# Compression and attention-gate weights read unsplit, as plain fp32 on four 32-column groups of the array

## What is computed

```python
DEPTH = 2
for l in range(DEPTH):
    h = rms_norm_2(x, norm_mix_pre[l])
    proj = h @ w_in[l]
    a_q, a_kv, a_gate, d_q, d_kv, b_in, c_in = jnp.split(proj, splits, axis=-1)
    ...
    k_cmp = nsa_compress(kv[:, :, 0, 0], nsa_cmp_pos[l, 0], nsa_cmp_w1[l, 0], nsa_cmp_w2[l, 0])
    v_cmp = nsa_compress(kv[:, :, 0, 1], nsa_cmp_pos[l, 1], nsa_cmp_w1[l, 1], nsa_cmp_w2[l, 1])
    o_cmp, p_cmp = nsa_compressed_attention(qa, k_cmp, v_cmp)
    ...
    ga = jax.nn.sigmoid(a_gate)          # 24 columns: 3 kinds x 8 heads
    o_a = ga[:, :, 0] * o_cmp + ga[:, :, 1] * o_slc + ga[:, :, 2] * o_win

def nsa_compress(k, pos, w1, w2):        # 15 blocks of 32 keys, stride 16, 2 key groups
    blk = k[:, idx] + pos
    flat = blk.reshape(bsz, n_cmp, g, 32 * 64)
    return gelu(flat @ w1) @ w2          # w1 is 2048 x 256
```

## Time and profile before

| | |
|---|---|
| median of three runs | 2051.24 us (2049.7 to 2053.11) |
| profiled execution, span | 2053.3 us |
| TensorE matmul busy | 2039.6 us, 99% |
| VectorE busy | 1475.2 us, 72% |
| ScalarE busy | 1152.8 us, 56% |
| chain that ended last | TensorE 96%, VectorE 1%, ScalarE 1%, DMA 1% |
| mean DMA rate | 180 GB/s |

### The profile page before, as it was taken

The page is one execution under the profiler, slowest core; times in us unless marked ns, Lnnn a source line. Parts: engine busy times, 40 slices in busy tenths (PEclk is TensorE's granted clock), DMA queues, the critical chain, the costliest instruction groups (busy, mean ns, idle before and its releaser), DMA issues.

```text
span 2053.3 us, 39877 instructions
## 1 busy us (share of the span) xinstructions
PE 2039.6 (99%) x17337; PEld 1975.7 (96%) x17340; DVE 1475.2 (72%) x1877; ACT 1152.8 (56%) x1459; POOL 129.9 (6%) x114
## 2 busy tenths in 40 slices
PE   9999999999999999999999999999999999999998
PEld 8999899999999999999999999999999999999998
DVE  6556866655655587676557999678778899868776
ACT  5435365534544456564446776756557685756555
POOL 1001000100101010010000000001000000000100
PEclk9999999999999999999999999999999999999999
DMA  7665544666566565366665554455655564445652
GB/s 256 206 206 175 183 144 141 196 198 195 175 207 200 190 193 165 103 200 221 223 200 168 163 165 140 159 175 186 223 191 156 162 199 160 149 151 171 222 186 103
DMA packets 287106, 369.78 MB, mean 180 GB/s; under 512 B 10531, under 2 KB 258771, under 8 KB 286931
## 3 DMA queue, kind: packets, MB, share of 16 engines
q1 hardware_dynamic: 281858, 361.47, 54.1%
q10 hardware_dynamic: 5072, 5.75, 0.9%
HBM read 365.36 MB, written 1.05 MB: 178 GB/s over the span
## 4 chain that ended last, share of the span: by engine, by line
PE 96%; DVE 1%; ACT 1%; DMA 1%; ACTq 0%; issue 0%; DVEq 0%
PE ps L717 28%; PE ps L718 27%; PE ps L719 27%; PE ps L828 1%; PE ps L889 1%; PE ps L887 1%; PE ps L885 1%; PE ps L1259 1%; PE ps L830 1%; PE ps L829 1%; DMA arena<-arena 1%; PE ps L1271 1%; PE ps L1292 1%; ACT whi L1482 1%; PE ps L1079 1%; PE ps L1106 0%
## 5 line engine op out<-in xcount | busy, mean ns | idle before, releaser
L717 PE MATMUL ps<-hhi,whi 128*128 128x256 f32 x3774 | 1056.2, 280 | 1.4 <-DVE hlo L2221 1.3
L718 PE MATMUL ps<-hlo,whi 128*128 128x256 f32 x3774 | 1044.1, 277 | 0.0
L719 PE MATMUL ps<-hhi,wlo 128*128 128x256 f32 x3774 | 1044.0, 277 | 0.0
L2128 DVE TENSOR_TENSOR wlo<-raw,whi 128x2048 fp32r<-128x2048 f32 x341 | 771.9, 2264 | 376.6 <-ACT whi L1482 376.5
L1482 ACT ACTIVATE whi<-raw 128x2048 fp32r<-128x2048 f32 (+2 forms) x346 | 651.4, 1886 | 537.1 <-PE ps L719 441.9
L717 PEld LDWEIGHTS ps<-hhi,whi 128*128 128x128 f32 x3774 | 707.6, 187 | 9.0 <-issue 5.4
L718 PEld LDWEIGHTS ps<-hlo,whi 128*128 128x128 f32 x3774 | 707.7, 188 | 1.2 <-issue 0.5
L719 PEld LDWEIGHTS ps<-hhi,wlo 128*128 128x128 f32 x3774 | 708.0, 188 | 0.2
L717 PE MATMUL ps<-hidhi,whi 128*128 128x256 f32 x880 | 243.3, 276 | 0.0
L719 PE MATMUL ps<-hidhi,wlo 128*128 128x256 f32 x880 | 243.1, 276 | 0.0
L718 PE MATMUL ps<-hidlo,whi 128*128 128x256 f32 x880 | 243.1, 276 | 0.0
(11 more groups left out here) (321 smaller groups left out, 2189.6 us busy)
## 6 DMA issues: line engine op xcount, KB each, us to landing
raw<-in_ffn_w_up SPq DMA_DIRECT2D x88, 1024.0 KB, 5.2
raw<-in_w_in SPq DMA_DIRECT2D x68, 1024.0 KB, 5.2
raw<-in_ffn_w_down SPq DMA_DIRECT2D x66, 1024.0 KB, 5.0
raw<-in_ffn_w_gate SPq DMA_DIRECT2D x43, 1024.0 KB, 5.3
raw<-in_w_gate SPq DMA_DIRECT2D x32, 1024.0 KB, 5.4
raw<-in_w_branch SPq DMA_DIRECT2D x16, 1024.0 KB, 5.0
raw<-in_nsa_cmp_w SPq DMA_DIRECT2D x8, 1024.0 KB, 5.4
raw<-in_w_out SPq DMA_DIRECT2D x6, 1024.0 KB, 5.0
```

The costliest lines, as they stand in the source:

```text
L717: pe.matmul(o, w_hi, m_hi, start=start, stop=False, skip_group_check=True)
L718: pe.matmul(o, w_hi, m_lo, start=False, stop=False, skip_group_check=True)
L719: return pe.matmul(o, w_lo, m_hi, start=False, stop=stop, skip_group_check=True)
L2128: dve.tensor_tensor(wlo[:, slot, 0:n], raw[:, slot, 0:n], whi[:, slot, 0:n].bitcast(F32), ALU.subtract) \
```

## The change

Units 14 to 18 (`PLAIN_UNITS`) are no longer split. TensorE multiplies with `raw` itself, in plain fp32. The eight blocks of a unit are spread over four groups of 32 columns of the array: block j goes to group j mod 4, whose sum lands in the partitions 32 q to 32 q + 31 of the same bank. For the gates the tokens stay split (`hhi`, `hlo`), two plain matmuls for a block; for the compression weights the block is read unsplit from `blkf`, one plain matmul for a block. The four partial sums are added by the matmul that turned the result anyway: with `quads`, four identities of 32 above one another, in place of the identity. For the hidden rows this has to come before the gelu, so ScalarE copies the rows first (126 partitions) and applies the gelu behind the turn. A load into a slot that held an unsplit unit waits until TensorE has used that unit. The split of the block goes too, and `pool_avg` moves, since `blkf` is now read for longer.

```diff
+PLAIN_UNITS = tuple(range(M2_AG, M2_GATE))
...
+            def load2(l, s, n, src):
+
+                slot = s % RING
+                if s - RING in PLAIN_UNITS:
+                    sp.wait_ge(used[slot], uses2(l, s))
+                    sp.dma_start(raw[:, slot, 0:n].rearrange("p (k c) -> p k c", k=src.shape[1]), src) \
+                        .then_inc(raw_ready[slot], 16)
+                else:
+                    load(slot, n, splits2(l, s), src)
...
                     v, part = divmod(i - M2_W1, 2)
                     if i == M2_W1:
-                        pe.wait_ge(blk_split, (l + 1) * 2)
-                    slot = i % RING
-                    unit_ready(slot, u(i))
-                    o = bank(4, v * CMP_HID, CMP_HID)[0:KVH * NCMP, :]
+                        pe.wait_ge(blk_ready, (l + 1) * BLK_STEPS)
+                    slot, rows = i % RING, KVH * NCMP
+                    pe.wait_ge(raw_ready[slot], 16 * (uses2(l, i) + 1))
                     for jl in range(CJ // 2):
-                        j = part * (CJ // 2) + jl
-                        w = slice(jl * CMP_HID, (jl + 1) * CMP_HID)
-                        b = slice(j * KVH * NCMP, (j + 1) * KVH * NCMP)
-                        last = mm3(o, blk_hi[:, v, b], blk_lo[:, v, b], whi[:, slot, w], wlo[:, slot, w], j == 0, j == CJ - 1)
+                        j, q = part * (CJ // 2) + jl, jl % 4
+                        n = QUAD if q < 3 else rows
+                        b = (v * CJ + j) * rows
+                        last = pe.matmul(bank(4, v * CMP_HID, CMP_HID)[q * QUAD:q * QUAD + n, :], blk_flat[:, b:b + n],
+                                         raw[:, slot, jl * CMP_HID:(jl + 1) * CMP_HID], start=j < 4, stop=j >= CJ - 4,
+                                         skip_group_check=True)
                     last.then_inc(used[slot], 1)
...
-                    pe.wait_ge(gelu_done, l * 3 + 1)
+                    pe.wait_ge(hid_kept, l + 1)
                     n = KVH * NCMP
                     for x in range(4):
-                        last = pe.matmul(bank(4, x * 32, n), hid_tok[0:n, x * P:(x + 1) * P], ident[0:n, 0:n], start=True, stop=True)
+                        last = pe.matmul(bank(4, x * QUAD, n), hid_tok[0:HID_ROWS, x * P:(x + 1) * P], quads[0:HID_ROWS, 0:n],
+                                         start=True, stop=True)
...
                         if i == M2_AG:
-                            for k in range(KC):
-                                w = slice(k * 3 * NSA_H, (k + 1) * 3 * NSA_H)
-                                last = mm3(bank(b, 0, SEQ)[0:3 * NSA_H, :], whi[:, slot, w], wlo[:, slot, w], hhi[:, k, :],
-                                           hlo[:, k, :], k == 0, k == KC - 1)
+                            pe.wait_ge(raw_ready[slot], 16 * (uses2(l, i) + 1))
+                            for k0 in (0, 4):
+                                for h in (hhi, hlo):
+                                    for q in range(4):
+                                        k, rows = k0 + q, QUAD if q < 3 else 3 * NSA_H
+                                        last = pe.matmul(bank(b, 0, SEQ)[q * QUAD:q * QUAD + rows, :],
+                                                         raw[:, slot, k * 3 * NSA_H:k * 3 * NSA_H + rows], h[:, k, :].bitcast(F32),
+                                                         start=k0 == 0 and h is hhi, stop=k0 > 0 and h is hlo, skip_group_check=True)
...
                 def next_split(i):
-                    n = {M2_AG: KC * 24, M2_OUT: D, M2_OUT + 1: D}.get(i + 2, UNIT)
+                    if i + 2 in PLAIN_UNITS:
+                        return
+                    n = {M2_OUT: D, M2_OUT + 1: D}.get(i + 2, UNIT)
...
                     if i == CMP_AT:
                         act.wait_ge(used[(CMP_AT - 1) % RING], uses2(l, CMP_AT - 1) + 1)
-                        act.activation(hid_tok[0:KVH * NCMP, :], bank(4)[0:KVH * NCMP, :], ACT.Gelu_apprx_tanh).then_inc(gelu_done, 1)
+                        act.activation(hid_tok[0:HID_ROWS, :], bank(4)[0:HID_ROWS, :], ACT.Copy).then_inc(hid_kept, 1)
...
                         act.wait_ge(hid_turned, l + 1)
                         act.activation(ghid.rearrange("p v m g n -> p (v m) g n")[:, :, :, 0:NCMP],
                                        bank(4, 0, P).rearrange("p (x n) -> p x n", x=4)[:, :, 0:KVH * NCMP]
-                                       .rearrange("p x (g n) -> p x g n", g=KVH), ACT.Copy).then_inc(gelu_done, 1)
-                        act.wait_ge(gelu_done, l * 3 + 2)
+                                       .rearrange("p x (g n) -> p x g n", g=KVH), ACT.Gelu_apprx_tanh).then_inc(gelu_done, 1)
+                        act.wait_ge(gelu_done, l * 2 + 1)
```

More of the change, by code:

```diff
@@ L54 @@
 CP = 16
+QUAD = 32
 CJ = CMP_LEN // 2
@@ L88 @@
 POOL_AT = 15
-BLK_AT = 9
 CONV_FROM = 7
@@ L164 @@
                       ("causal", 3 * P), ("window", 3 * P), ("cmpadd", TT * CP), ("cmp01", TT * CP),
-                      ("blockdiag", P), ("half", 2)])
+                      ("blockdiag", P), ("half", 2), ("quads", QUAD)])
 POOL_COLS = SEQ + P
@@ L225, in shape_consts @@
     half = (r[:, None] // DH) == np.arange(2)[None, :]
-    c2 = np.concatenate([cos, sin, *dup, *causal, *window, cmpadd, cmp01, blockdiag, half, *pool], 1)
+    quads = (r[:, None] % QUAD) == np.arange(QUAD)[None, :]
+    c2 = np.concatenate([cos, sin, *dup, *causal, *window, cmpadd, cmp01, blockdiag, half, quads, *pool], 1)
     return (np.eye(P, dtype=np.float32), np.ascontiguousarray(c1, np.float32), np.ascontiguousarray(c2, np.float32))
@@ L339, in hybrid_network @@
         cpad = view(m2["cpad"], c=BRC, t=CONV_PAD + SEQ)
-        blkf = view(gates.rearrange("p c t -> p (c t)")[:, 16 * SEQ - 2 * CJ * 2 * NCMP:], v=2, j=CJ, g=KVH, n=NCMP)
-        blk_hi, blk_lo = (x.rearrange("p b c t -> p b (c t)")[:, :, 0:CJ * 2 * NCMP] for x in (hidhi, hidlo))
+        blk_flat = gates.rearrange("p c t -> p (c t)")[:, 16 * SEQ - 2 * CJ * KVH * NCMP:]
+        blkf = view(blk_flat, v=2, j=CJ, g=KVH, n=NCMP)
         conv_acc = sq
@@ L387, in hybrid_network @@
         on_half = table(C2_AT, "half", 2)
+        quads = table(C2_AT, "quads", QUAD)
         def par_rows(i, r, n, src):
@@ L526, in uses2, with splits2, unsplit @@
             return DEPTH * (L1_UNITS // RING) + l * (L2_UNITS // RING) + s // RING
+        def splits2(l, s):
+            def unsplit(before):
+                return sum(x % RING == s % RING for x in PLAIN_UNITS if x < before)
+            return uses2(l, s) - l * unsplit(L2_UNITS) - unsplit(s)
         def bank1_of(i):
@@ L626, in conv_load @@
                 def conv_load(s, src):
-                    load(s % RING, UNIT, uses2(l, M2_END + s), src)
+                    load2(l, M2_END + s, UNIT, src)
                 def gate(p):
@@ L695, in _ @@
                                 .rearrange("k p c -> p k c")
-                        load(s % RING, UNIT, uses2(l, s), src)
+                        load2(l, s, UNIT, src)
                         s += 1
@@ L1436, in mixer2 @@
                         for t in range(TT):
-                            last = pe.transpose(bank(7, t * 3 * NSA_H, 3 * NSA_H), ga_rows[0:3 * NSA_H, t * P:(t + 1) * P],
-                                                ident[0:3 * NSA_H, 0:3 * NSA_H])
+                            last = pe.matmul(bank(7, t * 3 * NSA_H, 3 * NSA_H), ga_rows[0:GA_ROWS, t * P:(t + 1) * P],
+                                             quads[0:GA_ROWS, 0:3 * NSA_H], start=True, stop=True)
                         last.then_inc(ga_raw, 1)
```

67 lines of the change are left out of this document (30 added, 37 removed).

## The result

The changed kernel takes 2053.85 us (median of 21 executions, 2050.37 to 2057.79), the kernel before 2051.09 us on the same chip (21 executions, 2049.48 to 2057.02). The ratio is 1.0014, with a 95% interval of 1.0008 to 1.002: 2.8 us slower, where 1.6 us faster was forecast. It lies within the range and the 0.2% that the prediction named, but the sign is the other one; that the time fell into the range is owed to room that was left for other cases, two groups' rate above all.

The account below looks back on a forecast made before the run. TensorE, busy 99% of the span, was taken as the bound; load 19 cut 8.1 us a layer to 1.65, and one clock fall left 1.65 in all: 2051.24 - 1.65 = 2049.6, written 2049.5 us, range 2044 to 2058.

Parts of the forecast that it names:

- the 0.2%: Whole kernel: 4.1 us, about what a measurement can tell from no change; within it was given 0.61.
- two groups' rate: Rival, changed units: array fed for two groups only, 1.75 us a compression unit; 2055.7 us, chance 0.17.
- Four groups side by side: Changed units on TensorE: four column groups run at once, compression unit 0.88 us, gate unit 1.73 us.
- The plain sum: TensorE, changed units: 14.1 - (1.73 + 4 x 0.88 + 0.75) = 8.1 us a layer, which would be 2035 us.
- What is late next: Load 19, freed by unit 16's use, idles TensorE 4.2 us at `times_v(0)`; gain 1.65 us a layer, not 8.1.
- The landing of load 19: Load 19, issued at 1172.5, lands at about 1178.1, behind load 18 by 1175.2, at 2.9 us for 1 MB.
- The clock: Behind the `times_v(0)` wait: half clock takes a layer's gain to about 0.0 us; one fall likeliest, 2049.6 us, 0.30.
- two falls: Case of the main forecast: the clock falls twice over both layers, 2051.2 us, chance 0.14.
- Carry-over to the median: Profiled span 2053.3 us taken as 2 us above the median 2051.24; difference carried over, 2051.24 - 1.65 = 2049.6.
- loads in the open: Rival, changed units: four 0.03 us weight loads before every round delay load 19 by 1.7 to 1.9 us; 2051, chance 0.05.
- one after the other: Rival, changed units: groups run serially, 3.5 us a compression unit, 6.9 the gate unit; 2073 us, chance 0.03.
- the load doesn't bind: Rival: load 19 lands earlier or ScalarE's order is looser than read; 2047 to 2035 us, chance 0.11.

Follow-up runs that it names:

- c_room: Changed kernel with unit 16 read from the idle mixed-output buffer and load 19 sent ahead of load 16: 2041.67 us, ratio 0.9955 to the kernel before.
- b_order: Changed kernel with ScalarE's copy of load 19 moved behind the pooled output's scaling and VectorE's subtraction behind denominators(1): ratio 0.9983 to the kernel before.
- a_warm: Changed kernel with twenty matmuls of zeros ahead of the wait of `times_v(0)`, to keep TensorE busy: ratio 0.9998 to the kernel before.
- f_u16: Changed kernel with unit 16's matmuls moved directly behind unit 15's: ratio 1.001 to the kernel before.
- d_w1only: Changed kernel with only the compression weights plain on four groups, the gate weights split at 24 columns as before: ratio 1.0029 to the kernel before.
- j_ownfwd: Changed kernel with the gate weights in 192 columns of their own and unit 16's matmuls directly behind unit 15's: ratio 0.9971 to the kernel before.
- e_room2: c_room with ScalarE's copy of load 19 behind normalize(0) and the hidden rows' copy ahead of load 21's: 2040.61 us, ratio 0.9948 to the kernel before.

## Why the prediction was wrong, step by step

- **Four groups side by side: right.** 0.88 us a compression unit and 1.73 for the gate unit were forecast; to the next start they take 0.97 to 1.06 with the change of tiling, and 1.75. A round of four records takes 0.216 us (0.24 where it follows another tiling), and the four begin 1 to 7 ns apart. The rule weighed in the prediction (the Trainium skill, TensorE: Matmul & The Clock Gate, Part 3: a weight load overlaps running matmuls only when the row group differs) does not describe this kernel: all four groups use all 128 rows, and their loads cost nothing visible between the rounds.
- **The plain sum: 8.1 us a layer, some 7.1 found.** In c_room, up to the hidden turn, TensorE comes 5.0 us sooner than before (24.24 us against 29.21 from the gate unit's start), and three waits hold 2.15 us (0.87 and 0.90 shown above, 0.38 at the hidden turn): 7.1 us. Some 0.2 us of the rest is the gate turn, 0.76 us from 1167.99 to 1168.75 in the changed kernel where 0.41 stood before (1176.98 to the next step): 0.35 us more, of which I had put down 0.15. The rest is open.
- **What is late next: right in kind and place.** Loads 17, 18 and 19 were forecast 2.0, 2.9 and 7.5 us behind the gate unit's start and went out 2.0, 2.9 and 7.5 us behind it. One wait at `times_v(0)` in each layer, behind the tanh, behind the copy, behind the landing. b_order shows the link from the copy to the tanh, c_room the one from the slot to the landing.
- **The landing of load 19: mis-sized, 0.6 us.** Counted from the gate unit's start I had it land after 13.1 us (1178.1); it took 13.7. The forecast let load 17 fly 5.4 us and the next two land 2.8 and 2.9 us apart; load 17, first of a row, flew 5.7 us and the two behind it landed 3.0 us apart each. (The 357 GB/s behind the 2.9 us is not the queues' best stretch, as the earlier trace rows has it: the trace of before moved 379 GB/s from 930 to 936 us. The loads of this row are slower than that.) The wait was 4.9 us instead of 4.2, and `hidden_turn`'s 1.2 and 1.0 us instead of 0.3, as unit 18, which frees load 21's slot, came late and at half clock. Without the clock the change would have gained 0.6 and 0.95 us a layer (a_warm), not 1.65: 1.75 us of the 4.4 us between forecast and result.
- **The clock: the step that turned the sign.** The forecast had one fall in the two layers, 1.65 us. The profiled execution has one in each layer and a third behind the second wait; a_warm puts the cost at 4.1 us, 2.5 us more than forecast. The price of a fall was not too low (1.35 us in layer 1); their number was. The mean clock of all 21 executions (0.993 to 0.997) lies below that of each of the 23 executions of the kernel before that ran beside the first experiments (0.999 to 1.000), so the falls belong to the change. The error was in reading the one fall of the kernel before as a thing that may come or not behind a given wait, on the ground that its three runs lie 3.4 us apart. No clock is on record for those three, but those 23 have 0.999 or 1.000 and still vary by 3 us. What was rare was the wait: at the same place (L1079, L1102 in the changed kernel) the changed kernel waits 1.06 us and no experiment longer, and none has a fall there. With two falls, a forecast of 2051.2 us stood among the cases, at 0.14; even that is 2.8 us less than the change cost, as the second wait and its fall were missing.
- **Carry-over to the median: harmless.** The prediction set the span of the profiled execution (2053.3 us) against a median of times and found it 2 us above. In every execution with both on record the time is 1.8 us more than the span, so it lay some 4 us above. The forecast doesn't hang on it, since only the gain was carried over; but a span that holds a rare fall says nothing of how many falls the median has.
- **The rivals.** Two groups' rate (2055.7 us) is not what happened, though its time is near; the records refute it, and so they do loads in the open and one after the other. That the load doesn't bind is refuted for the change as it is; c_room shows what it would have been worth.

## What to carry to other kernels

Work that is taken away from the busiest engine is worth only what the next resource allows, and that is found by asking who frees each buffer: a split stage that looks like pure overhead may be what frees the load's slot early (load 19's by 4.4 us here, 1172.58 against the end of unit 16 at 1176.98). Set a late transfer against everything that stands behind its consumer in program order, not only against the unit that needs the data, and count loads that go out together at the spacing that such loads have in a trace, not at the flight time of one alone. If a forecast leaves a wait of several microseconds on TensorE, price the halved clock with it (each of the 13 waits of 2.2 us or more in these traces had a fall), not as a chance; and look for the one buffer that breaks the chain: here it made the difference between a loss of 2.8 us and a gain of 9 us (c_room).

## What the runs showed of the hardware that was not expected

- Plain fp32 matmuls of 256 columns on four groups of 32 columns, each with its own stationary data on all 128 rows, run four records at a time in 0.216 us, the time of one record on the whole array, though each group also has its own moving data. It is so in the gate unit and in the compression units.
- Loads of 1 MB of the gate and compression weights that stand in one queue land 2.8 to 3.0 us apart, whenever they were issued: third of three 9.8 us after its issue (f_u16), second of two mostly 7.5 to 8.3, first or alone mostly 5.2 to 5.8. The rate is that of these loads and not of the queue: in the changed kernel the load of branch weights behind them lands 2.5 us after the one before it (1190.19 and 1192.71), and it moves in larger packets. That the packets are the cause is not shown.
- The clock fell at every one of the 13 waits of 2.2 to 5.6 us (the 3.57 us of the kernel before among them), for 3.4 or 6.8 us. It fell again behind waits of 1.0 to 1.9 us at the hidden turn that came some 10 us after such a fall (changed kernel in layer 0, d_w1only and f_u16 in both), but not behind the 0.99 us in layer 1 of the changed kernel. It did not fall at the 0.9 and 0.9 us of c_room nor at the 1.1, 1.5 and 0.9 us within 10 us of j_ownfwd. Two falls of 3.4 us came without such a wait: the second in layer 0 of b_order, and one in e_room2 at the start, behind a wait of 1.3 us that all traces have and that brought a fall in this one alone.
